# A hybrid decoder layer on one core: projection stage in another order, sample values in more buffers

## What is computed

```python
n = rms_norm(x, norm_g)
u, q, k, v = split(n @ w_in)                 # 512 columns each
q, k = rms_norm(heads(q), g_q), rms_norm(heads(k), g_k)      # 8 heads of 64
pool_o = pool_mixer(u, history, ...)         # causal means over 2, 4, 8, 16 rows, one product per group
z = q @ k.T * 64 ** -0.5 + bias; log_keep = log_sigmoid(-z) where visible
a = exp(log_sigmoid(z) + later(log_keep)); attn = a @ v      # "stick breaking"
x = x + concat(pool_o, attn) @ w_out
x = x + hier_moe(rms_norm(x))                # router, 2 of 32 experts per row, silu gate
```

## Time and profile before

| | us |
|---|---|
| runs of the kernel before | 1191.54, 1192.58, 1196.94 |
| their median | 1192.58 |
| the profiled execution | 1194.32 |
| its span, first to last instruction | 1192.6 |
| TensorE busy | 1102.7 (92%) |
| TensorE weight load busy | 796.5 (67%) |
| DVE busy | 439.5 (37%) |
| ACT busy | 329.0 (28%) |
| POOL busy | 173.2 (15%) |
| DMA rate over the span | 250 GB/s, 297.60 MB |
| mean granted TensorE clock | 0.967 |

### The profile page before, as it was taken

How to read it: one execution, slowest core, us unless ns; L and a number is a source line. 1 busy time by engine, 2 the same in 40 slices (tenths; PEclk the granted TensorE clock), 3 DMA queues, 4 the chain that set the end, 5 groups by cost and what they waited for, 6 DMA issues and landing times.

```text
span 1192.6 us, 26688 instructions
## 1 busy us (share of the span) xinstructions
PE 1102.7 (92%) x11558; PEld 796.5 (67%) x11558; DVE 439.5 (37%) x803; ACT 329.0 (28%) x642; POOL 173.2 (15%) x149
## 2 busy tenths in 40 slices
PE   3999799999999979999869999999999999989985
PEld 3999799975766538899646666666666655556543
DVE  3424555329875541545522122212222221212211
ACT  4422223136775543122201111111111111111111
POOL 0000210099500000000010111111111111111100
PEclk9999899999999998999769999999999999999988
DMA  6426777000106375565779999999999999999972
GB/s 192 126 66 173 222 246 230 1 13 1 37 1 213 106 247 187 175 241 231 285 266 385 370 383 374 371 374 378 381 374 369 374 381 382 378 368 380 376 279 48
DMA packets 84832, 297.60 MB, mean 250 GB/s; under 512 B 11394, under 2 KB 42818, under 8 KB 59096
## 3 DMA queue, kind: packets, MB, share of 16 engines
q1 hardware_dynamic: 77543, 274.48, 62.2%
q0 software_dynamic: 7168, 21.37, 7.9%
HBM read 272.98 MB, written 43.66 MB: 266 GB/s over the span
## 4 chain that ended last, share of the span: by engine, by line
PE 77%; DMA 13%; DVE 5%; ACT 2%; issue 2%; SPq 1%; POOL 0%; ACTq 0%; POOLq 0%; DVEq 0%
PE bank L1993 10%; DMA w_ring<-in_w_up 9%; PE bank L2377 9%; PE bank L2381 8%; PE bank L2233 8%; PE bank L2385 7%; PE bank L2411 4%; PE bank L2045 4%; PE bank L2415 4%; PE bank L2419 3%; PE bank L2210 3%; PE bank L2174 3%; PE bank L2083 2%; PE bank L2356 2%; DMA out_k_all<-kn 2%
## 5 line engine op out<-in xcount | busy, mean ns | idle before, releaser
L2377 PE MATMUL bank<-w_ring,xeT 128*32 128x256 f32 x1536 | 351.4, 386 | 0.0
L2381 PE MATMUL bank<-w_ring,xeT 128*32 128x512 f32 x1536 | 272.9, 607 | 14.3 <-DMA w_ring<-in_w_up 13.6
L2377 PEld LDWEIGHTS bank<-w_ring,xeT 128*32 128x32 f32 x1536 | 168.4, 112 | 56.3 <-issue 3.7
L2411 PE MATMUL bank<-w_ring,hT 128*32 128x256 f32 x768 | 171.7, 380 | 0.0
L2385 PE MATMUL bank<-w_ring,xeT 128*32 128x256 f32 x1536 | 159.2, 385 | 0.0
L1879 DVE SCALAR_TENSOR_TENSOR hid<-sgl,gtab,bank 96x256 f32<-96x256 f32 x32 | 21.9, 683 | 358.8 <-ACT sgl L1439 358.8
L2415 PE MATMUL bank<-w_ring,hT 128*32 128x512 f32 x768 | 133.2, 595 | 1.6 <-ACT hT L1445 1.6
L1993 PE MATMUL bank<-w_hi,xh 128*128 128x256 f32 (+1 forms) x432 | 126.1, 292 | 2.5 <-DVE xl L1501 2.4
L1993 PE MATMUL bank<-w_lo,xh 128*128 128x256 f32 (+1 forms) x432 | 123.0, 285 | 0.0
L1993 PE MATMUL bank<-w_hi,xl 128*128 128x256 f32 (+1 forms) x432 | 122.9, 284 | 0.0
L1628 DVE TENSOR_TENSOR_SCAN keep<-keep,unseen 128x1024 f32<-128x1024 f32 (+7 forms) x64 | 94.7, 1512 | 51.1 <-ACT keep L1239 50.9
(11 more groups left out here) (259 smaller groups left out, 1621.5 us busy)
## 6 DMA issues: line engine op xcount, KB each, us to landing
w_ring<-in_w_gate SPq DMA_DIRECT2D x64, 1024.0 KB, 28.6
w_ring<-in_w_up SPq DMA_DIRECT2D x64, 1024.0 KB, 28.4
w_ring<-in_w_down SPq DMA_DIRECT2D x64, 1024.0 KB, 32.7
w_raw<-in_w_in SPq DMA_DIRECT2D x8, 1024.0 KB, 7.5
k_scr<-in_cache_k SPq DMA_DIRECT2D x32, 256.0 KB, 3.8
v_scr<-in_cache_v SPq DMA_DIRECT2D x32, 256.0 KB, 3.5
pgk<-k_scr SPq DMA_DIRECT2D x32, 256.0 KB, 3.9
pgv<-v_scr SPq DMA_DIRECT2D x4, 1024.0 KB, 6.3
```

What stands on the lines that cost most here:

```text
L2377: return pe.matmul(up_right_ps(i, g), xeT[i][:, k, rows_of(g)], w[1][:, k, FA:F], start=first and g != 1, stop=ends, skip_group_check=True)
L2381: pe.matmul(gate_ps(i)[rows_of(g), :], xeT[i][:, k, rows_of(g)], w[0][:, k, :], start=first, stop=ends, skip_group_check=True)
L2411: return pe.matmul(y_right_ps(g), hT[:, ft, rows_of(g)], w[:, ft, DA:D], start=first and g != 1, stop=ends, skip_group_check=True)
```

## The change

- Start: ACT takes one root of a constant before data arrive, so its function table is loaded then. Root 0 stands ahead of square 1. The first weights come as two halves of 512 KB, the first ahead of x tile 1, each split for itself; the counts of `s_whi` and `s_wlo` are one higher from there on, and product 0 waits for the second half at slice 4.
- Rows: odd tiles are transposed into banks 6 and 7, even ones into 0 and 1, and a tile's transposes wait for the copies of the tile two before. Tile t + 2 is transposed directly after v step t. In the stages root and scaling stand ahead of the high and low copies.
- SP: one page copy a step from step 10 on, and the last 20 behind the loop. The wait for the page table stands ahead of step 0. The shifted load of tile 0 is two loads of 15 and 112 rows.
- u: products 0, 1 and 2 stand between the last head transposes, in banks 4, 5, 2, product 3 in bank 3; the history is transposed after them.
- Sample values: eight loads with places of their own in turn (`pgv0`, v rows of tiles 4 to 7, `pgv2` over the first key buffer, `pgv0`, `kTs[0]`, `kTs[1]`, the v rows, `pgv0`), four semaphores, and loads 2 to 5 asked for before w_out's first part, 6 and 7 after it. The high half of w_out's first part waits for page 2 to be summed.

```diff
+    pgv += [place("pgv2", [PAGE, SQ, AW], F32, at_k[0])[0], pgv[0], kTs[0], kTs[1], pgv[1], pgv[0]]
...
+    def rows_ps(t):
+        b = 6 * (t % 2)
+        return bank[:, b:b + 2, :].rearrange("p b (c n) -> p (b c) n", n=P)
...
+    PAGE_FROM = 10
...
-        return bank[:, 4 + (s - NS) % 2, :]
+        return bank[:, (4, 5, 2, 3)[s - NS] if s < NS + 4 else 4 + (s - NS) % 2, :]
...
-                    sp.wait_ge(s_whi, n - 1)
-                    sp.wait_ge(s_wlo, n - 1)
-                sp.dma_start(w_raw[n % 2][:, :, :], w_in_v[:, :, c:c + CG]).then_inc(s_wld[n % 2], 16)
+                    sp.wait_ge(s_whi, n)
+                    sp.wait_ge(s_wlo, n)
+                loaded = s_hld if k.stop < KT else s_wld[n % 2]
+                sp.dma_start(w_raw[n % 2][:, k, :], w_in_v[:, k, c:c + CG]).then_inc(loaded, 16)
...
-                    sp.dma_start(dst[1:P, :], v_all[0:P - 1, :]).then_inc(loaded, 16)
+                    sp.dma_start(dst[1:16, :], v_all[0:15, :]).then_inc(loaded, 16)
+                    sp.dma_start(dst[16:P, :], v_all[15:P - 1, :]).then_inc(loaded, 16)
...
+            load_w(0, slice(0, KT // 2))
             load_x(1)
-            load_w(0)
+            load_w(0, slice(KT // 2, KT))
             load_x(2)
...
-            pages = 0
+            sp.wait_ge(s_pt, 16)
...
-                if s >= NV:
-                    while pages < min(2 * DB * NPG, 2 * (s - NV + 1)):
-                        copy_page(pages)
-                        pages += 1
+                if s >= PAGE_FROM:
+                    copy_page(s - PAGE_FROM)
+
+            for n in range(NS - PAGE_FROM, 2 * DB * NPG):
+                copy_page(n)
...
-                if n >= 2:
-
-                    sp.wait_ge(s_avs, SQ * (n - 1))
                 src = v_scr[SQ * g:SQ * g + SQ, c].rearrange("b p f -> p b f")
-                sp.dma_start(pgv[n % 2][:, :, :], src).then_inc(s_vld[n % 2], 16)
+                sp.dma_start(pgv[n][:, :, :], src).then_inc(s_vld[n % NPG], 16)
...
+            sp.wait_ge(s_t, turned("keys", NKEY - 2, SQ - 1))
+            load_values(2)
+            sp.wait_ge(s_avs, SQ)
+            load_values(3)
+            sp.wait_ge(s_zp, SQ * (NKEY - 1))
+            load_values(4)
+            sp.wait_ge(s_zp, SQ * NKEY)
+            sp.wait_ge(s_avs, SQ * 2)
+            load_values(5)
             sp.wait_ge(s_t, turned("keys", NKEY - 1, SQ - 1))
-            for n in range(2, NPG):
-                load_values(n)
...
-            for n in range(NPG, NSG * NPG):
-                load_values(n)
+            sp.wait_ge(s_avs, SQ * 3)
+            load_values(6)
+            sp.wait_ge(s_avs, SQ * 4)
+            load_values(7)
...
+            act.wait_ge(s_ident, 1)
+            act.activation(hr[:, 0, 0:1], one_col[:, :], ACT.Sqrt)
             square(0)
-            norm_stages(0)
+            root(0)
+            act.wait_ge(s_hld, 16)
+            act.activation(w_hi[0][:, 0:KT // 2, :], w_raw[0][:, 0:KT // 2, :], ACT.Copy).then_inc(s_whi, 1)
+            square(1)
+            root(1)
+            hi_rows(0)
             split_hi(0)
-            norm_stages(1)
+            square(2)
...
-                    act.wait_ge(s_t, turned("keys", NKEY - 1, SQ - 1))
+                    act.wait_ge(s_avs, SQ * 3)
...
             mean_square(0)
-            norm_stages(0)
+            norm_rows(0)
+            dve.wait_ge(s_whi, 1)
+            dve.tensor_tensor(w_lo[0][:, 0:KT // 2, :], w_raw[0][:, 0:KT // 2, :], w_hi[0][:, 0:KT // 2, :].bitcast(F32),
+                              ALU.subtract).then_inc(s_wlo, 1)
+            mean_square(1)
+            norm_rows(1)
+            lo_rows(0)
             split_lo(0)
-            norm_stages(1)
+            mean_square(2)
...
-                else:
-
-                    pe.wait_ge(s_xh, t)
-                    pe.wait_ge(s_xl, t)
+                if t >= 2:
+
+                    pe.wait_ge(s_xh, t - 1)
+                    pe.wait_ge(s_xl, t - 1)
...
+            for s in range(NS + 3):
+                if s < NS:
+                    project(s)
+                    if steps[s][0:2] == ("v", 0) and steps[s][2] + 2 < NT:
+                        transpose_x(steps[s][2] + 2)
+                else:
+                    project_u(s - NS)
+                if NV + 3 <= s < NS + 3:
+                    transpose_heads(s - 3 - NV)
+
+            transpose_history()
+            for i in range(3, NUS - 1):
```

More of the change, by code:

```diff
@@ L517, in hybrid_step @@
     s_kld = [sem(f"k_pages_loaded{i}") for i in range(2)]
-    s_vld = [sem(f"v_pages_loaded{i}") for i in range(2)]
+    s_vld = [sem(f"v_pages_loaded{i}") for i in range(NPG)]
     s_qz = sem("q_spread")
@@ L985, in _ @@
             chain = Chain(pool, s_pool)
+            chain.link(pool.memset(one_col[:, :], 1.0))
             chain.link(pool.memset(ident[:, :], 1.0))
@@ L1156, in square, with root, hi_rows @@
                                accum_out=ss[0:r, t % 2:t % 2 + 1]).then_inc(s_ssq, 1)
+            def root(i):
+                act.wait_ge(s_ms, i + 1)
+                if i >= 2:
+                    act.wait_ge(s_xs, i - 1)
+                act.activation(rs[0:ROWS[i], i % 2:i % 2 + 1], ss[0:ROWS[i], i % 2:i % 2 + 1],
+                               ACT.Sqrt).then_inc(s_rms, 1)
+            def hi_rows(t):
+                r = ROWS[t]
+                act.wait_ge(s_xT, t + 1)
+                act.activation(xh[:, :, row0(t):row0(t) + r], rows_ps(t)[:, :, 0:r], ACT.Copy).then_inc(s_xh, 1)
             def norm_stages(i):
[L1160 to L1164, removed]
+                if i < NT:
+                    root(i)
+                if i <= NT:
+                    hi_rows(i - 1)
                 if i + 1 < NT:
                     square(i + 1)
[L1167 to L1173, removed]
             def split_hi(n):
@@ L1179, in split_hi @@
                     act.wait_ge(s_pr, ends[n - 2])
[L1180 removed]
+                k = slice(KT // 2 if n == 0 else 0, KT)
+                act.activation(w_hi[n % 2][:, k, :], w_raw[n % 2][:, k, :], ACT.Copy).then_inc(s_whi, 1)
+            act.wait_ge(s_ident, 1)
+            act.activation(hr[:, 0, 0:1], one_col[:, :], ACT.Sqrt)
             square(0)
[L1183 removed]
+            root(0)
[4 more added lines that the diff above has]
+            hi_rows(0)
             split_hi(0)
[L1185 removed]
+            square(2)
             for s in range(NS + 4):
@@ L1493, in mean_square, with norm_rows, lo_rows @@
                 dve.tensor_scalar(ss[0:ROWS[t], c], ss[0:ROWS[t], c], 1.0 / D, EPS, ALU.mult, ALU.add).then_inc(s_ms, 1)
-            def norm_stages(i):
[L1497 to L1502, removed]
-                if i < NT:
[L1504 to L1508, removed]
+            def norm_rows(i):
+                r, c = ROWS[i], slice(i % 2, i % 2 + 1)
+                dve.wait_ge(s_rms, i + 1)
+                chain.link(dve.reciprocal(rs[0:r, c], rs[0:r, c]))
+                dve.scalar_tensor_tensor(out=xt[i % 3][0:r, :], in0=xt[i % 3][0:r, :], scalar=rs[0:r, c],
+                                         in1=gmix[0:r, :], op0=ALU.mult, op1=ALU.mult).then_inc(s_xs, 1)
+            def lo_rows(t):
+                r = ROWS[t]
+                dve.wait_ge(s_xh, t + 1)
+                dve.tensor_tensor(xl[:, :, row0(t):row0(t) + r], rows_ps(t)[:, :, 0:r],
+                                  xh[:, :, row0(t):row0(t) + r].bitcast(F32), ALU.subtract).then_inc(s_xl, 1)
+            def norm_stages(i):
+                if i < NT:
+                    norm_rows(i)
+                if i <= NT:
+                    lo_rows(i - 1)
                 if i + 1 < NT:
@@ L1991, in project @@
                 for k in range(KT):
+                    if s == 0 and k == KT // 2:
+                        pe.wait_ge(s_whi, 2)
+                        pe.wait_ge(s_wlo, 2)
                     for j, (a, b) in enumerate(((xh, w_hi), (xh, w_lo), (xl, w_hi))):
@@ L2004, in transpose_heads @@
                 last.then_inc(s_kt, 1)
-            transpose_x(0)
-            transpose_x(1)
-            for s in range(NS + 3):
-                if s < NS:
-                    project(s)
-                    if s >= 1 and steps[s - 1][0:2] == ("v", 0) and steps[s - 1][2] + 2 < NT:
-                        transpose_x(steps[s - 1][2] + 2)
-                if NV + 3 <= s < NS + 3:
-                    transpose_heads(s - 3 - NV)
             def transpose_history():
-                pe.wait_ge(s_hld, 16)
+                pe.wait_ge(s_hld, 32)
                 pe.wait_ge(s_ke, NQK)
@@ L2035, in project_u @@
                 if i == 0 or i == NUS // 2:
-                    pe.wait_ge(s_whi, n + 1)
-                    pe.wait_ge(s_wlo, n + 1)
-                if i < 2:
-                    pe.wait_ge(s_kn, NQK)
+                    pe.wait_ge(s_whi, n + 2)
+                    pe.wait_ge(s_wlo, n + 2)
+                if i < 4:
+                    pe.wait_ge(s_kn, NQK - 3 + i)
                 else:
```

(11 more changed lines are left out.)

21 lines of the change are left out of this document (10 added, 11 removed).

## The result

The changed kernel takes **1158.65 us** (median of 4 runs, 1156.52 to 1163.11) against 1192.06 of the kernel before beside it (4 runs): ratio **0.9718**, 95% interval 0.9678 to 0.9758. The profiled execution took 1158.96 with a span of 1157.2, where before it was 1194.32 and 1192.6. The forecast was 1160 with a range of 1153 to 1170, so the time is within 1.4 of it.

What follows compares the result with a forecast made beforehand. Expert weight stream sets the end but starts with TensorE's progress, so TensorE time saved before 460 us counts: 7.0 + 14.4 + 4.4 + 7.5 = 33.3 off 1194.3 gives 1161, 1159 against the median; 1160 taken, range 1153 to 1170.

Steps and rivals of the forecast that it cites:

- The start: Load, scaling and transposes up to the v steps: earlier table load and reordering save 7.0 us, bounds 4 to 8.
- P3: Product 3 of the v steps: forecast to end at 31.3, where the same work ended at 38.33 before.
- the upper bound of 8: Start: the gain in us if SP's new wait for the page table costs nothing.
- k and q steps: Stalls for normed heads behind late k stores, with their clock loss, go: 14.4 us saved, bounds 7 to 14.8.
- Rival (b): k and q steps: only crowded page copies cause stalls, not the 127 rows; half a stall stays, 1167 us; chance 0.07.
- Rival (a): k and q steps: w loads still stall the k store at steps 23 and 32, 3.4 each, 1167 us; chance 0.12.
- Turn: From the last q product to the u projections: waits filled by u products, 4.4 us saved, bounds 2.5 to 5.1.
- Sample values: End of attention: late value pages 3, 6 and 7 come in time, 7.5 us saved, bounds 3 to 8.5.
- The 3.7 for the clock: Sample values: 5.2 us of lower-clock time lost at 440 to 460, less 1.5 hidden by idle time, is regained.
- Rival (c): Start gives only 4 and sample values only 3, as both lean on queue landing times: 1168 us; chance 0.15.
- Rival (d): v steps: each tile's norm chain binds, costing 48 us against 33 saved: slower, 1207 us; chance 0.03.
- Expert stage: Paced by its weight stream, forecast as long as before, moving earlier by what TensorE saves before 460 us.

Runs made afterwards that it cites:

- e8: Changed kernel with SP's page-table wait moved from ahead of step 0 to right before the first page copy at step 10; 1160.26 us, ratio 0.9742.
- e7: Changed kernel without the root of a constant ahead of the loads; 1163.12 us, ratio 0.9787.
- e10: Changed kernel with each tile transposed one product later, as before, its two buffers kept; 1159.32 us, ratio 0.9755.
- e2: Changed kernel with the shifted load of tile 0 as one load of 127 rows again; 1165.06 us, ratio 0.9771.
- e4: Kernel before with one page copy a step from step 10, the last 20 behind the loop, 127-row load kept; 1181.38 us, ratio 0.9914.
- e1: Kernel before with only the shifted load of tile 0 split into parts of 15 and 112 rows; 1185.33 us, ratio 0.9929.
- e3: Changed kernel with two page copies a step from step 18 on, two-part load kept; 1167.51 us, ratio 0.9797.
- e9: Changed kernel with the page-table wait at step 10 and DVE's low half of w_out's first part two attention units later; 1156.57 us, ratio 0.9722.
- c1: The changed kernel itself, unaltered, run once more against the kernel before; 1158.54 us, ratio 0.9735.
- e5: Changed kernel with two sample-value buffers and the old order of loads; 1165.33 us, ratio 0.9797.
- e11: Changed kernel with late page-table wait, later low half of w_out's first part, and x tile 1 ahead of the first weights; 1159.22 us, ratio 0.9743.

## Why the prediction was right, step by step

The terms are compared as measured against forecast, each in the stretch of the table that holds it.

**The start, 7.0 against 7.0.** The size is right and so are the marks: the first product was to start at 14.8 and did at 14.67; P3 was to end at 31.3, and ends at 31.34 (T4 at 27.43, then one product from 28.52). Two steps of its reasoning are wrong. "That lets x4 be issued at 17.4 and land at about 20.7" named the page-table wait as a cause; e8 takes it away and nothing moves, so the upper bound of 8, "if that wait costs nothing", doesn't exist either. The rest of that sentence, w 1's halves ahead of tile 4's scaling, carries the hole by itself; that is read from rows, no run moves them. And "the change loads the table before data arrive" gave an edit a place in the argument that is worth nothing on TensorE (e7). My own working had it: scaling 1, set by x1, ended at 12.8, whatever tile 0 did. What brings the first product 5.0 forward is that root and scaling of tile 1 stand ahead of tile 0's copies: DVE scales it at 11.71, and in before at 16.71, behind the low half of w 0 and tile 0's low rows. That is read from the rows; no run takes this order back alone. Turning each tile one product earlier is tested, and worth about 1.5 (e10).

**k and q steps, 14.3 against 14.4.** Both named causes are real. Taking the load of 127 rows away gives 6.7 in before, and putting it back costs 6.8 in after; for the page copies it is 9.4 and 7.1. They are not a sum of one stall each: what they give alone adds up to 16.1 from before, more than the 14.3 that there is. Part of that is the clock: e2 and e4 have the same queue in these steps and stalls of 3.9 and 3.4, but 6.8 us at the lower clock in one and 3.4 in the other, and their step lengths differ by 1.9. Rival (b), that the 127 rows are no cause, falls by e1 and e2. Rival (a), a stall behind the load of weights, did not come, but closely: the store took 8.1 where I took 6.89 from the earlier trace rows, against an estimated slack of 8.2 ("k stores over 8 us" was even to count as a sign of error), and DVE waited 1.4. With two pages a step (e3) that stall is there twice.

**Turn, 4.9 against 4.4.** The history wait is there, 0.43 where 0.45 was forecast. The 0.3 for ACT's copies ahead of u3 is not: the trace shows no other hole between 190 and 215. The remaining 0.2 is as much as the history's transposes got shorter, 0.58 in before and 0.37 in after, which the working leaves out.

**Sample values, 7.3 against 7.5.** All pages came in time, w_out's first part did not, as forecast ("up to 1.5 late"): it landed 1.1 late and held ACT, then DVE, then TensorE.

```profile
407.95 1.91 ACT L1391 ACTIVATE wo_hi<-wo_raw 128x2048 fp32r<-128x2048 f32 x1 [1.09 <-DMA wo_raw<-in_w_out]
409.90 2.29 DVE L1715 TENSOR_TENSOR wo_lo<-wo_raw,wo_hi 128x2048 fp32r<-128x2048 f32 x1 [5.06 <-ACT wo_hi L1391]
412.11 1.36 DVE L1671 TENSOR_TENSOR_SCAN keep<-keep,unseen 128x128 f32<-128x128 f32 x4
412.99 0.41 PE L2210 MATMUL bank<-ident,keep 128*128 128x128 f32 x2 [1.17 <-DVE keep L1671]
```

It costs 1.17 where I took 1.0, and through DVE's queue: e9 leaves the load 1.23 late and only moves the low half, and TensorE doesn't wait. The 3.7 for the clock was sound for the execution that was profiled, but not a property of the kernel: see below. That the term came out within 0.2 is partly luck, for the changed kernel itself took 1.7 more in this stretch in c1. Rival (c), 4 and 3 for these two terms, falls with both. Rival (d), a norm chain that binds the v steps, is seen at tile 4 alone, and costs 1.2.

**Expert stage.** As long as before to 1.0 us, with the DMA share at 1.02: what TensorE saved ahead of 460 arrived at the end whole, and 1.8 more, which the forecast put at nothing. That is inside the spread of this stage. So the mechanism of the four terms is in the main the forecast one, but that the sum before 460 agrees to 0.2 and the time to 1.4 is closer than two executions of one kernel agree (1156.5 to 1163.1 for after).

## What to carry to other kernels

Where a queue is late, look for two things apart: a transfer with an unlucky number of rows (127 here, where 128, and 15 and 112, were quick), which holds everything behind it and the issuing engine too, and an issuing engine whose work per step is longer than the step (3.65 against 3.04 here). Take each away alone before adding their gains. An operation moved off a chain is worth nothing while another chain ends later at the same consumer: tile 1 behind its load here, not tile 0 behind the table.

## What I had not expected of the hardware

**The moment at which the clock rises is not fixed to the first product.** In after the matmuls of the first product drop from 0.41 to 0.28 at 17.2:

```profile
16.95 0.39 PE L2039 MATMUL bank<-w_lo,xh 128*128 128x256 f32 x1
17.17 0.30 PE L2039 MATMUL bank<-w_hi,xl 128*128 128x256 f32 x1
17.30 0.28 PE L2039 MATMUL bank<-w_hi,xh 128*128 128x256 f32 x1
```

With nearly the same start it was 16.1 in e8, 16.3 in e9, 18.15 in c1 and 18.4 in e5. The first head transposes follow it by about half the difference: 84.78, 84.97, 85.36 (after), 85.78, 85.93. So e8's and e9's lead of 0.4 to 0.6 there is this and no work of the edits, and e11, whose first product began 0.76 earlier than e9's, had its rise 1.2 later (17.53), which costs 0.6: together with the 0.76, which at half the clock is worth 0.4, it explains the 0.18 by which e11 was behind at the head transposes. Against e8, with a rise only 0.4 later, e10 lost 1.7, of which 0.2 is the clock: the later transposes cost about 1.5.

**Small waits don't always lower the clock.** Near the sample values before shows 4.0 + 0.8 of waits (longest 2.5) and then 10.2 us at the lower clock. Before with one page a step (e4) shows 3.8 + 0.8 in the same places, longest 2.0, and none:

```profile
PE bank L2153 <- DMA vv<-v_scr: 3.8, 2, 2.0
...
440.00:460.00 20.00, 19.64 (x165) 18.75 (x164) 2.01 (x6) 5.38 (x5) 0.00 (x0) 1.00 0.56 186
```

e5 waits 4.1 + 0.5 and gets 6.8 us of it. After's own stall of 1.17 passes without, while the same kernel in c1, stalled 1.23 at 413.49, has 3.4 us from 414.2 and reads 0.91 in its window from 400 to 420. In the output product each of these kernels has a stall of 1.2 to 2.0; behind it e8 (stall 2.0) and e5 (1.9) get 3.4 us of the lower clock, while e2 (1.8) and before (1.8) get none. A term priced by the lower clock in one execution can thus be off by some 3 us in the next. What decides between them is open.
